# Compressed units first in the first attention, no identity products in its steady part, and eight dot-product tiles moved to the first feed-forward

## The chip, the cores and the metric

One core of one Trainium2 chip runs the whole program. The metric is the device time of one execution in microseconds (us); three executions of the kernel before are known. Engines are named as in the profile: PE is TensorE, DVE VectorE, ACT ScalarE, POOL GpSimd, SP the SyncE queue that issues the DMAs.

## The reference, cut to what matters

The program is two blocks. The first is one hybrid attention layer over 512 tokens; the second is two layers (feed-forward, mixer, feed-forward) over 512 + 256 tokens, modulated by vectors that come from a condition.

```python
# first block, for one layer
o_cmp, p_cmp = compressed_branch(qn, kc_cmp, vc_cmp)   # 31 compressed keys
o_sel = selected_branch(qn, ks_r, vs, sel_idx)
o_win = window_branch(qn, kw_r, vw)
o_nsa = (g0 * o_cmp + g1 * o_sel + g2 * o_win) * silu(z_n)
o_dsa = dsa_branch(qd, kd, v_d, qi_r, ki_r, wi) * silu(z_d)  # top 128 keys by an index score
x = x + concatenate([o_nsa, o_dsa]) @ w_out

# second block, for layer i
m  = split(silu(c)     @ w_ada[i] + b_ada[i], 9)       # 9 vectors of 1024
mc = split(silu(c_ctx) @ w_ada[i] + b_ada[i], 9)
h  = h + 0.5 * m[2] * swiglu(rms_norm(h) * (1 + m[1]) + m[0], w13, w2)
...
```

## The kernel before, in words

Each engine has its own instruction list and runs it strictly in order; semaphores tie them. Blocks end with a barrier of all engines. The blocks that the change touches come in this order: `compress` makes the compressed keys and values, `index_scores` makes the scores of the last branch (dsa), `attend_first` is the attention, `first_out` projects, and the first call of `ffn` follows.

**The attention** works through 16 units. A unit is one tile of 128 queries with one branch, for 8 heads. The branches cmp, sel and win of tile 3 come first, then those of tiles 2, 1 and 0, then the four dsa units. A unit has `items`, one for each group of 4 heads and each tile of 128 keys; a cmp unit has two, of 32 keys. For an item PE makes two products of 512 columns (three with a mask), `score`; ACT takes the exponential; PE multiplies with the values, 4 products, `weigh`. `weigh` of the item before is woven between the products of `score`. The row maxima must be there first: PE makes the rows (`row`, one product for each head, or 8 small ones in one go for a cmp unit), DVE reduces them (`maxes`), PE transposes the maxima (`turn`), ACT moves them (`move`), POOL spreads them (`spread_max`). Rows are made three units ahead: those of the first three units in a prologue, those of unit i+3 during unit i, shared out over its items, through two PSUM banks in turn (`wait_bank`), so that row j+2 waits until DVE has reduced row j.

DVE runs for each unit i: `finish(i - 1)`, `maxes(i + 3)`, then `rounds_at[i]` rounds of `topk` (48 rounds in all: 16 each for scores of 256, 384 and 512 keys; each round finds eight maxima and replaces them), then `share.vector`. Identity products (`keep_warm`) write to unused columns of PSUM: one after each row of the prologue, and one before the third product of each `weigh`.

**The modulation** vectors are dot products on DVE (`AdaShare`). A tile is 512 KB of `w_ada`, loaded to one of two buffers, and two products of 128x1024 (one for each condition); 72 tiles are one layer. 16 tiles are in `compress`, 8 in `attend_first`, 48 in the first `ffn`. `AdaShare.load` has SP wait, for tile n, until tile n-2 is done (`ada.SLOTS` is 2), and what SP has queued behind waits as well. `finish` adds the bias and the gain.

**The feed-forward** runs 34 steps, each of two weight loads of 512 KB. For step s ACT rounds the weights, DVE makes the rest (`rest_next`), PE multiplies. In iteration s DVE first makes the rest of step s+1, then takes the results of step s, then does its tiles of the share. On SP the order is: weights of step s, then the share's tiles of step s-1, then the weights of step s+1.

Of the kernel before, what the change touches and what calls it, by code (L numbers as in the profile page):

```python
# [6 lines left out]
P = 128  # L7
# [835 lines left out]
def compress(c, T, KKc, KLc, Vc, dram, share):  # L843
# [9 lines left out]
    with scope(nc) as sb:  # L853
# [14 lines left out]
        with nc.Block() as block:  # L868
# [22 lines left out]
            def _(pe):  # L891
# [14 lines left out]
                for g in range(GROUPS):  # L906
                    for ht in range(HT):
                        last = nc.tensor.matmul(c.PS[0:CMP_PAD, 5, g * HD:(g + 1) * HD], hid[:, 1, ht, g, :], w2[:, 1, ht, :], start=(ht == 0), stop=(ht == HT - 1))
                last.then_inc(out_done.sem, 1)
                pe.wait_ge(normed.sem, 1)  # L910
                for g in range(GROUPS):
# [67 lines left out]
def index_scores(c, rows, Q, KK, KL, scores, tri, sc_at, dram):  # L979
# [4 lines left out]
    with scope(nc) as sb:  # L984
        R = sb("ix_r", [P, 2, SEQ])
        wi = sb("ix_w", [P, QT, IDX_HEADS])
        with nc.Block() as block:
# [5 lines left out]
            def _(pe):  # L993
                for n, (t, h) in enumerate(items):
                    if n >= 4:
                        pe.wait_ge(relu.sem, n - 3)
                    keys = (t + 1) * P
                    tok = slice(t * P, (t + 1) * P)
                    half = slice(HD * (h % 2), HD * (h % 2) + HD)
                    q = HEAD_AT["qi"] + h  # L1000
                    nc.tensor.matmul(c.PS[:, n % 4, 0:keys], Q[:, q, tok], KK[:, KI_AT, 0:keys], start=True, stop=False)
                    nc.tensor.matmul(c.PS[:, n % 4, 0:keys], Q[half, q, tok], KL[half, KI_AT, 0:keys], start=False, stop=True
                                     ).then_inc(scored.sem, 1)

            @block.scalar
# [39 lines left out]
def attend_first(c, sb, rows, O, Q, KK, KL, KKc, KLc, Vx, Vc, scores, sc_at, tri, dram, share):  # L1045
# [5 lines left out]
    nc = c.nc  # L1051
    units = [FirstUnit(t, b) for t in range(QT - 1, -1, -1) for b in ("cmp", "sel", "win")] + [FirstUnit(t, "dsa") for t in range(QT)]
    n_units = len(units)
    rounds_at = [3, 8, 8, 2, 6, 6, 2, 4, 4, 1, 2, 2]
    rounds = [(t, r) for t in range(1, QT) for r in range(TOPK // 8)]
# [46 lines left out]
    with nc.Block() as block:  # L1102
        @block.sync
        def _(sp):
            sp.dma_start(negeye[:], dram["neg_eye"]).then_inc(tabs, 16)
            sp.dma_start(cneg[:], dram["cmp_neg"]).then_inc(tabs, 16)
            for i in range(n_units):
                share.load(sp, i)
            ring = Ring(c)
# [3 lines left out]
        def _(pe):  # L1113
# [51 lines left out]

            def keep_warm(bank, first=False):
                nc.tensor.matmul(c.PS[:, bank, 3 * P:4 * P], c.ident[:], c.ident[:], start=first, stop=True, skip_group_check=True)

            def weigh(n):
# [5 lines left out]
                for h in range(PER_GROUP):  # L1175
                    if h == 2:
                        keep_warm(o_bank(i, g))
                    if u.branch == "cmp":
# [8 lines left out]
                yield  # L1187

            for i in range(3):
                for j in range(units[i].row_items):  # L1190
                    row(i, j)
                    keep_warm(4 + j % 4, True)
                if i >= 1:
# [117 lines left out]
        def _(dve):  # L1311
            ch = c.dve.on(dve)

            def maxes(i):
# [3 lines left out]
                for j in range(u.row_items):  # L1318
                    dve.wait_ge(rowed, row_first[i] + j + 1)
                    ps = c.PS[:, bank("row", i, j), 0:u.keys]  # L1320
                    if u.branch == "cmp":
                        ps = c.PS[:, bank("row", i, j), 0:HEADS * CMP_PAD].rearrange("p (h c) -> p h c", h=HEADS)
                        ch.link(nc.vector.tensor_tensor(Sc[:], ps, cneg[:, u.t, None, :].to_broadcast([P, HEADS, CMP_PAD]), ALU.add))
                        nc.vector.reduce_max(Mx[:, i % 3, :, 64:68], Sc[:].rearrange("p (g h) c -> p g h c", g=GROUPS), AX_X).then_inc(maxed, 1)
# [48 lines left out]
            for i in range(n_units):  # L1373
# [4 lines left out]
                if i < len(rounds_at):  # L1378
                    for n in range(done, done + rounds_at[i]):
                        topk(n)  # L1380
                    done += rounds_at[i]
                share.vector(dve, ch, i)
            finish(n_units - 1)
# [367 lines left out]
class AdaShare:  # L1751
# [46 lines left out]

    def finish(self, dve, ch):

        ada, nc = self.ada, self.ada.nc
        if not self.finish_list:
            return
        dve.wait_ge(ada.small_in, 32)
        dve.wait_ge(ada.done, self.tiles[-1].stop)
        mods = [(l, v, m) for l, m in self.finish_list for v in range(2)]
        at = lambda l, v, m: ada.c.mod[:, l, v, m * KT:(m + 1) * KT]
# [12 lines left out]
def first_block(c, dram):  # L1820
    nc = c.nc
    O = c.hT.rearrange("p k n -> p (k n)")[:, 0:QT * D].rearrange("p (t n) -> p t n", t=QT)
    with scope(nc) as sb1:
# [9 lines left out]
        with scope(nc) as sb2:  # L1833
            KKc, KLc = sb2("KKc", [P, GROUPS, CMP_PAD], F32R), sb2("KLc", [P, GROUPS, CMP_PAD], F32R)
            Vc = sb2("Vc", [CMP_PAD, GROUPS, 66])
            s_c, room = sb2("ada_s", [P, 2, D]), sb2("ada_room", [P, 3, D])
            share = AdaShare(c.ada, s_c, [room[:, 0], room[:, 1]], room[:, 2], [2] * 8, [])
            compress(c, T, KKc, KLc, Vc, dram, share)
# [4 lines left out]
            with scope(nc) as sb:  # L1843
                later = AdaShare(c.ada, s_c, share.bufs, share.product, [0, 1, 1, 0, 1, 1, 0, 0, 0, 0, 0, 0, 1, 1, 1, 1], [(0, m) for m in range(3)], share)
                attend_first(c, sb, rows, O, Q, KK, KL, KKc, KLc, Vx, Vc, scores, sc_at, tri, dram, later)

# [152 lines left out]

def ffn(c, sb, ring, x, w13, w2, gates, spans, tag, after=None, shares=None, finish=()):  # L2000

# [48 lines left out]
    with nc.Block() as block:  # L2050
# [111 lines left out]
        def _(dve):  # L2162
# [5 lines left out]
            def body(s1, f0, is_up, i, more, opened=False):  # L2168
                for s, half, q, k in two(s1, i):
# [25 lines left out]
                    if share:  # L2195
                        share.vector(dve, c.dve.on(dve), s - s0)

            x.vector(dve, c.dve.on(dve), ring.rest_second(dve, s0))
# [570 lines left out]

def ada_shares(up, down):  # L2770

    out = []
    for f in range(0, FT, 8):
        out += [up] * min(8, FT - f) + [down if f == 0 else 0] * (KT // 2)
    return out


ADA_PLAN = {(0, 0): (ada_shares(2, 1), [(0, m) for m in range(3, 9)]),
            (0, 1): ([1] * 24, [(1, m) for m in range(3)]),
# [161 lines left out]
```

## Time and profile before

| | us |
|---|---|
| median of 3 executions | 3452.81 |
| lowest, highest | 3432.56, 3461.04 |
| the profiled execution, its own time | 3457.02 |
| its span (first to last instruction) | 3454.9 |
| mean granted TensorE clock | 0.935 |

Everything below is read from the profiled execution. A time without a unit is in us from the start of the span; the granted clock is 1.00 at 2.4 GHz and 0.50 at 1.2 GHz.

### The profile page before, as it was taken

Reading aid. Unit: us, or ns where it says so; the run is one execution under the profiler, and the core shown is the slowest. Engines: PE = TensorE matmul, PEld = TensorE weight load, DVE = VectorE, ACT = ScalarE, POOL = GpSimd, SP = SyncE. Lnnn points to the kernel's source line nnn. Section 1 sums busy time; section 2 is a strip of 40 time slices with the busy share of each in tenths; the row PEclk is TensorE's granted clock in tenths of the full one; section 3 lists DMA queues with packets and bytes.
Section 4 is the critical chain, followed back from the end, with each engine's and each line's share of the span. In section 5 each row is a group of like instructions: output and inputs, shape, how many; then the busy total and the mean of one; then the engine's idle time right before and its main releaser. Section 6 shows DMA issues by size and latency. Waiting matters only on the chain. (4 is left out here: it accounts for less than half of the span.)

```text
span 3454.9 us, 43440 instructions
## 1 busy us (share of the span) xinstructions
PE 3259.5 (94%) x18372; PEld 2819.4 (82%) x18372; DVE 1803.5 (52%) x2690; ACT 839.4 (24%) x1019; POOL 127.1 (4%) x96
## 2 busy tenths in 40 slices
PE   7847989899999999989999999999999999899999
PEld 6746878788888888668888888888888886699997
DVE  4656464276463663653644543664654556554434
ACT  3312222241121231222311212321211132132222
POOL 2320122000000000000000000000000000000000
PEclk9975555899999999999999999999999999999999
DMA  4332001234242412112333221343433320233331
GB/s 140 91 117 89 13 13 37 86 113 149 81 130 75 125 52 62 29 54 62 104 103 91 91 74 58 89 128 103 122 110 85 94 60 17 69 92 94 92 89 58
DMA packets 340322, 288.36 MB, mean 83 GB/s; under 512 B 12896, under 2 KB 315488, under 8 KB 339168
## 3 DMA queue, kind: packets, MB, share of 16 engines
q1 hardware_dynamic: 340192, 286.58, 28.3%
q8 instruction: 88, 1.44, 0.2%
q14 instruction: 42, 0.34, 0.0%
HBM read 279.72 MB, written 2.10 MB: 82 GB/s over the span
## 5 line engine op out<-in xcount | busy, mean ns | idle before, releaser
L2117 PE MATMUL PS<-x_hi_f,w_lo 128*128 128x258 f32 (+2 forms) x2560 | 622.3, 324 | 0.0
L2117 PE MATMUL PS<-x_lo_f,w_hi 128*128 128x258 f32 (+2 forms) x2560 | 622.0, 324 | 0.0
L2117 PE MATMUL PS<-x_hi_f,w_hi 128*128 128x258 f32 (+2 forms) x2560 | 620.9, 323 | 0.8 <-DVE w_lo L2165 0.8
L2117 PEld LDWEIGHTS PS<-x_hi_f,w_hi 128*128 128x128 f32 x2560 | 395.4, 189 | 43.9 <-issue 1.5
L2117 PEld LDWEIGHTS PS<-x_hi_f,w_lo 128*128 128x128 f32 x2560 | 395.3, 189 | 42.0
L2117 PEld LDWEIGHTS PS<-x_lo_f,w_hi 128*128 128x128 f32 x2560 | 393.2, 189 | 40.5
L2132 ACT ACTIVATE w_hi<-w_raw 128x2048 fp32r<-128x2048 f32 x131 | 250.0, 1909 | 498.6 <-PE PS L2117 496.7
L2117 PE MATMUL PS<-hid_hi_f,w_hi 128*128 128x512 f32 x1232 | 341.7, 347 | 0.9 <-DVE hid_lo_f L2185 0.9
L2117 PE MATMUL PS<-hid_hi_f,w_lo 128*128 128x512 f32 x1232 | 341.3, 347 | 0.0
L2117 PE MATMUL PS<-hid_lo_f,w_hi 128*128 128x512 f32 x1232 | 338.9, 345 | 0.0
L2165 DVE TENSOR_TENSOR w_lo<-w_raw,w_hi 128x2048 fp32r<-128x2048 f32 x131 | 299.6, 2287 | 35.1 <-ACT w_hi L2132 35.1
L2143 ACT ACTIVATE silu_a_f<-silu_a_f,shift_out_f 128x512 f32<-128x512 f32 (+1 forms) x154 | 90.2, 626 | 927.9 <-DVE silu_a_f L2176 927.9
L1793 DVE SCALAR_TENSOR_TENSOR sq_f<-sq_f,ada_s 128x1024 f32<-128x1024 f32 x240 | 293.5, 1223 | 8.8
L2192 DVE SCALAR_TENSOR_TENSOR hT<-PS,mod,hT 128x512 f32<-128x512 f32 (+1 forms) x168 | 95.8, 630 | 372.5 <-PE PS L2117 372.5
L2175 DVE COPY shift_out_f<-PS 128x4 f32<-128x4 f32 x88 | 14.3, 162 | 448.2 <-PE PS L2117 444.4
L2117 PEld LDWEIGHTS PS<-hid_hi_f,w_hi 128*128 128x128 f32 x1232 | 195.6, 188 | 33.0 <-DVE hid_lo_f L2185 2.3
L2117 PEld LDWEIGHTS PS<-hid_lo_f,w_hi 128*128 128x128 f32 x1232 | 194.9, 188 | 32.0
L2117 PEld LDWEIGHTS PS<-hid_hi_f,w_lo 128*128 128x128 f32 x1232 | 196.3, 188 | 28.9
L1182 PEld LDWEIGHTS PS<-first_v,exp_t 128*128 128x128 f32 x480 | 140.9, 331 | 11.7
L1182 PE MATMUL PS<-first_v,exp_t 128*128 128x66 f32 x480 | 123.5, 376 | 0.0
L2185 DVE TENSOR_TENSOR hid_lo_f<-hid_f_f,hid_hi_f 128x768 fp32r<-128x768 f32 (+1 forms) x88 | 78.5, 892 | 84.0 <-ACT hid_hi_f L2146 84.0
L139 PEld LDWEIGHTS PS<-ident 128*128 128x128 f32 x812 | 97.0, 196 | 20.0 <-issue 19.1
(325 smaller groups left out, 4607.1 us busy)
## 6 DMA issues: line engine op xcount, KB each, us to landing
w_raw<-in_w_ffn_dram SPq DMA_DIRECT2D x240, 512.0 KB, 5.1
sq_f<-in_w_ada_dram SPq DMA_DIRECT2D x120, 512.0 KB, 3.6
w_raw<-in_w_in_dram SPq DMA_DIRECT2D x46, 512.0 KB, 5.0
ada_room<-in_w_ada_dram SPq DMA_DIRECT2D x24, 512.0 KB, 3.5
w_raw<-in_w_out_dram SPq DMA_DIRECT2D x24, 512.0 KB, 5.2
w_raw<-in_w_ffn_dram SPq DMA_DIRECT2D x32, 384.0 KB, 3.9
ada_s<-in_conditions_dram SPq DMA_DIRECT2D x4, 1024.0 KB, 5.4
hT<-hT SPq DMA_DIRECT2D x56, 64.0 KB, 2.0
```

Of the source, the lines that this page charges most:

```text
L139: self.nc.tensor.matmul(self.PS[:, bank, 0:P], self.ident[:], self.ident[:], start=True, stop=True)
L1182: last = nc.tensor.matmul(c.PS[:, o_bank(i, g), h * 66:(h + 1) * 66], e, v, start=(kt == 0 and h == 0), stop=(kt == u.tiles - 1 and h == P ...
L1793: dot = nc.vector.scalar_tensor_tensor(self.product, self.bufs[n % ada.SLOTS], 1.0, self.s[:, v], ALU.mult, ALU.mult, accum_out=ada.c.mod[ ...
L2117: last = nc.tensor.matmul(c.PS[:, 4 * q + 2 * w + m, 0:e - a], wt, xt[:, a:e], start=first, stop=end)
L2132: nc.scalar.activation(ring.hi[:, q, :], ring.raw[:, q, :], ACT.Copy).then_inc(ring.rounded, 1)
L2143: last = nc.scalar.activation(sa[:, q, a:e], sa[:, q, a:e], ACT.Silu, bias=cc[:, q, 0, v:v + 1])
L2165: nc.vector.tensor_tensor(ring.lo[:, q, :], ring.raw[:, q, :], ring.hi[:, q, :].bitcast(F32), ALU.subtract).then_inc(ring.split, 1)
L2175: nc.vector.tensor_copy(cc[:, q], c.PS[:, 4 * q + 1:4 * q + 4:2, n_tok - cut:n_tok - cut + n_sh])
L2185: nc.vector.tensor_tensor(hid_lo[:, 2 * i + k, :], hf[:, q, :], hid_hi[:, 2 * i + k, :].bitcast(F32), ALU.subtract).then_inc(h_split.sem, 1)
L2192: last = nc.vector.scalar_tensor_tensor(c.hT[:, d, a:e], res(q, w)[:, a:e], gate[:, d:d + 1], c.hT[:, d, a:e], ALU.mult, ALU.add)
```

## The change

1. The four cmp units come first, then sel and win of tiles 3 to 0, then dsa. `rounds_at` goes from 3, 8, 8, 2, 6, 6, 2, 4, 4, 1, 2, 2 to none in the four cmp units and then 9, 10, 6, 7, 4, 4, 4, 4.
2. The identity product in `weigh` goes. In the prologue there are four after each row item, where there was one; since all three units there are cmp now, there are three row items and not 17.
3. 36 identity products stand in `compress` before PE waits for the normed keys, and 14 at the end of `index_scores`.
4. `attend_first` has no tile of the modulation; its eight are done in the first `ffn`, three in each of the first eight steps instead of two. The vectors 0 and 1 are finished at the end of the attention, vector 2 in step 3 of the `ffn`.
5. In `maxes` DVE waits for its own earlier maxima before it reuses `Sc`.

```diff
                 last.then_inc(out_done.sem, 1)
+                c.keep_warm(36, 7)
                 pe.wait_ge(normed.sem, 1)
...
                                      ).then_inc(scored.sem, 1)
+                c.keep_warm(14, 7)
...
-    units = [FirstUnit(t, b) for t in range(QT - 1, -1, -1) for b in ("cmp", "sel", "win")] + [FirstUnit(t, "dsa") for t in range(QT)]
+    units = [FirstUnit(t, "cmp") for t in range(QT - 1, -1, -1)]
+    units += [FirstUnit(t, b) for t in range(QT - 1, -1, -1) for b in ("sel", "win")] + [FirstUnit(t, "dsa") for t in range(QT)]
-    rounds_at = [3, 8, 8, 2, 6, 6, 2, 4, 4, 1, 2, 2]
+    rounds_at = [0, 0, 0, 0, 9, 10, 6, 7, 4, 4, 4, 4]
...
-            for i in range(n_units):
-                share.load(sp, i)
...
                 for h in range(PER_GROUP):
-                    if h == 2:
-                        keep_warm(o_bank(i, g))
...
                     row(i, j)
-                    keep_warm(4 + j % 4, True)
+                    for b in range(4, 8):
+                        keep_warm(b, True)
...
+                        if i >= 1:
+                            dve.wait_ge(maxed, row_first[i])
...
-                share.vector(dve, ch, i)
             finish(n_units - 1)
             share.finish(dve, ch)
...
-            share = AdaShare(c.ada, s_c, [room[:, 0], room[:, 1]], room[:, 2], [2] * 8, [])
+            share = AdaShare(c.ada, s_c, [room[:, 0], room[:, 1]], room[:, 2], [2] * 8, [(0, 0), (0, 1)])
...
-                later = AdaShare(c.ada, s_c, share.bufs, share.product, [0, 1, 1, 0, 1, 1, 0, 0, 0, 0, 0, 0, 1, 1, 1, 1], [(0, m) for m in range(3)], share)
...
                         share.vector(dve, c.dve.on(dve), s - s0)
+                        if soon and s - s0 == soon[0]:
+                            share.finish(dve, c.dve.on(dve), soon[1])
...
-        out += [up] * min(8, FT - f) + [down if f == 0 else 0] * (KT // 2)
+        out += [first if first and f == 0 else up] * min(8, FT - f) + [down if f == 0 else 0] * (KT // 2)
...
-ADA_PLAN = {(0, 0): (ada_shares(2, 1), [(0, m) for m in range(3, 9)]),
+ADA_PLAN = {(0, 0): (ada_shares(2, 1, 3), [(0, m) for m in range(3, 9)], (3, [(0, 2)])),
```

## Rows read from the trace of the kernel before

**Rows 1.** The page: the granted clock in 40 slices of the span

```profile
PEclk9975555899999999999999999999999999999999
```

**Rows 2.** Busy time by stretch (start:end, length, engines, granted clock, DMA share, GB/s)

```profile
330.20:343.60 13.40, 10.77 (x57) 7.47 (x55) 6.92 (x20) 8.65 (x14) 5.21 (x6) 1.00 0.00 1
...
408.60:412.00 3.40, 3.40 (x22) 2.52 (x21) 3.19 (x11) 1.84 (x4) 1.98 (x2) 0.99 0.00 0
...
542.00:624.60 82.60, 80.66 (x296) 71.03 (x295) 29.28 (x66) 15.83 (x27) 15.29 (x10) 0.50 0.15 39
```

**Rows 3.** Waits of PE from 345 to 626: who for whom, total, times, longest

```profile
PE PS L1124 <- DVE row_max L1333: 12.4, 8, 3.6
PE PS L1132 <- DVE row_max L1324: 7.0, 2, 4.0
```

**Rows 4.** Timeline of PE, 303 to 339 (start, length, instruction, idle before)

```profile
303.56 0.42 PE L912 MATMUL PS<-ident,cmp_r 32*128 32x32 f32 x2 [13.86 <-DVE cmp_r L969]
...
321.61 1.86 PE L1121 MATMUL PS<-KKc,Q 128*128 128x32 f32 x8 [1.74 <-PEq L987]
...
338.07 0.48 PE L1158 MATMUL PS<-Q,KKc 128*32 128x512 f32 x1
```

**Rows 5.** Timeline of PE, an item of the steady part

```profile
355.36 0.63 PE L1167 MATMUL PS<-ident 128*128 128x128 f32 x2
355.78 0.96 PE L1182 MATMUL PS<-first_v,exp_t 128*128 128x66 f32 x4
356.49 0.77 PE L1158 MATMUL PS<-Q,KK 128*128 128x512 f32 x1
357.07 0.53 PE L1182 MATMUL PS<-first_v,exp_t 128*128 128x66 f32 x2
```

**Rows 6.** Timeline of all engines, ACT and POOL in the prologue

```profile
327.69 3.90 ACT L1252 ACTIVATE first_rows<-first_rows 128x1024 f32<-128x1024 f32 x4
...
332.78 0.38 ACT L1233 ACTIVATE row_max_t<-PS 4x256 f32<-4x256 f32 x1
...
333.23 2.03 POOL L1278 TENSOR_TENSOR qr<-row_max_t,neg_eye 4x512 fp32r<-4x512 f32 x2 [113.37 <-ACT row_max_t L1233]
```

**Rows 7.** Timeline of DVE: last round on 256 keys, a tile, then finish

```profile
381.21 0.43 DVE L1338 MAX8 top<-scores 128x8 f32<-128x256 f32 x1
...
382.19 1.22 DVE L1793 SCALAR_TENSOR_TENSOR ada_room<-ada_room,ada_s 128x1024 f32<-128x1024 f32 x1
...
384.61 0.20 DVE L1349 RECIPROCAL co<-PS 128x8 f32<-128x8 f32 x1
```

**Rows 8.** Timeline of PE: its wait behind them

```profile
386.39 0.69 PE L1124 MATMUL PS<-KK,Q 128*128 128x384 f32 x1 [3.62 <-DVE row_max L1333]
```

**Rows 9.** Timeline of DVE: the starts of two rounds on 512 keys

```profile
492.11 0.69 DVE L1338 MAX8 top<-scores 128x8 f32<-128x512 f32 x1
...
493.63 0.69 DVE L1338 MAX8 top<-scores 128x8 f32<-128x512 f32 x1
```

**Rows 10.** Timeline of DVE: steps 1 and 3 of the first feed-forward

```profile
733.22 0.15 DVE L2175 COPY shift_out_f<-PS 128x4 f32<-128x4 f32 x1
...
767.52 0.16 DVE L2175 COPY shift_out_f<-PS 128x4 f32<-128x4 f32 x1 [4.30 <-PE PS L2117]
...
777.79 2.29 DVE L2165 TENSOR_TENSOR w_lo<-w_raw,w_hi 128x2048 fp32r<-128x2048 f32 x1
...
784.39 0.16 DVE L2175 COPY shift_out_f<-PS 128x4 f32<-128x4 f32 x1 [4.31 <-PE PS L2117]
```

**Rows 11.** Timeline of SP's queue, the same steps (start, from the first issue to the last)

```profile
775.29 2.95 SPq L1781 DMA_DIRECT2D sq_f<-in_w_ada_dram  x2
778.28 1.06 SPq L2061 DMA_DIRECT2D w_raw<-in_w_ffn_dram  x2
```

**Rows 12.** Source view of the feed-forward's weight loads (L2061), 726 to 850

```profile
DMA to landing us min/median/max: 5.0/5.8/6.9
```

**Rows 13.** Timeline of ACT, rounding of a step's weights

```profile
771.76 1.91 ACT L2132 ACTIVATE w_hi<-w_raw 128x2048 fp32r<-128x2048 f32 x1
```

More of the change, by code:

```diff
@@ L1164, in score @@
                 yield
-            def keep_warm(bank, first=False):
-                nc.tensor.matmul(c.PS[:, bank, 3 * P:4 * P], c.ident[:], c.ident[:], start=first, stop=True, skip_group_check=True)
             def weigh(n):
@@ L1187, in weigh, with keep_warm @@
                 yield
+            def keep_warm(bank, first=False):
+                nc.tensor.matmul(c.PS[:, bank, 3 * P:4 * P], c.ident[:], c.ident[:], start=first, stop=True, skip_group_check=True)
             for i in range(3):
@@ L1797, in vector, with finish @@
             dot.then_inc(ada.done, 1)
-    def finish(self, dve, ch):
+    def finish(self, dve, ch, some=None):
         ada, nc = self.ada, self.ada.nc
-        if not self.finish_list:
+        which = some or self.finish_list
+        if not which:
             return
         dve.wait_ge(ada.small_in, 32)
-        dve.wait_ge(ada.done, self.tiles[-1].stop)
-        mods = [(l, v, m) for l, m in self.finish_list for v in range(2)]
+        dve.wait_ge(ada.done, max(l * N_MOD * KT + (m + 1) * KT for l, m in which))
+        mods = [(l, v, m) for l, m in which for v in range(2)]
         at = lambda l, v, m: ada.c.mod[:, l, v, m * KT:(m + 1) * KT]
@@ L1843, in first_block @@
             with scope(nc) as sb:
-                later = AdaShare(c.ada, s_c, share.bufs, share.product, [0, 1, 1, 0, 1, 1, 0, 0, 0, 0, 0, 0, 1, 1, 1, 1], [(0, m) for m in range(3)], share)
-                attend_first(c, sb, rows, O, Q, KK, KL, KKc, KLc, Vx, Vc, scores, sc_at, tri, dram, later)
+                attend_first(c, sb, rows, O, Q, KK, KL, KKc, KLc, Vx, Vc, scores, sc_at, tri, dram, share)
 class Refill:
@@ L1997, in invert, with ffn @@
         ch.link(self.c.nc.vector.reciprocal(self.inv[:], self.inv[:]))
-def ffn(c, sb, ring, x, w13, w2, gates, spans, tag, after=None, shares=None, finish=()):
+def ffn(c, sb, ring, x, w13, w2, gates, spans, tag, after=None, shares=None, finish=(), soon=None):
     nc = c.nc
@@ L2767, in _, with ada_shares @@
                 sp.wait_ge(stored.sem, 16 * len(items))
-def ada_shares(up, down):
+def ada_shares(up, down, first=None):
     out = []
     for f in range(0, FT, 8):
-        out += [up] * min(8, FT - f) + [down if f == 0 else 0] * (KT // 2)
+        out += [first if first and f == 0 else up] * min(8, FT - f) + [down if f == 0 else 0] * (KT // 2)
     return out
-ADA_PLAN = {(0, 0): (ada_shares(2, 1), [(0, m) for m in range(3, 9)]),
+ADA_PLAN = {(0, 0): (ada_shares(2, 1, 3), [(0, m) for m in range(3, 9)], (3, [(0, 2)])),
             (0, 1): ([1] * 24, [(1, m) for m in range(3)]),
```

## The prediction

> **What bounds the kernel now.** I read the page's clock line first. TensorE has its full clock nearly everywhere except in the four slices from 259 to 605 us and at their edges [rows 1], and the first attention lies in the second half of that hole. Then the stretches. In the attention's last 82.6 us PE is busy for 80.66 at a clock of 0.50, which is 1.2 GHz; the clock is at 2.4 GHz only in the prologue and in short spells around a cmp unit [rows 2]. So the attention is bound by PE at half clock. What PE waits for there is DVE, and little of it: 12.4 us for row maxima of key tiles and 7.0 us, in two waits, for those of cmp units, 19.4 us together [rows 3]. The rest of the program, from 700 us on, is a feed-forward that PE bounds at full clock. There a step is 784.39 - 767.52 = 16.87 us, and DVE has 4.31 us of each step to spare [rows 10].
>
> **The change part by part.** Sums are made against the profiled execution: 3457.02 us, 2.1 of them outside its span. It stands 4.2 us above the median, 3452.81.
>
> *Identity products in compress.* PE idles 13.86 us before the transposes [rows 4]. One product (two records) takes 355.78 - 355.36 = 0.42 us at half clock [rows 5], so 36 take 15.1 us at that rate and half of it, 7.6, at the full one. The clock can't stay low through all of them if the prologue is a guide (it rose there while rows and identity products ran back to back), so they lie in the gap. Cost 0; up to 1.2 if the clock never rises. What follows them is idle again, so I give them no gain.
>
> *Identity products after the index scores.* 14 x 0.42 = 5.9 us, or 2.9 at full clock. PE's last product there ends 1.74 us before the attention's first [rows 4], and DVE covers most of that gap. The attention begins later by 1.5 to 4.7; I take +4.
>
> *The prologue.* Its length was the time from 321.61 to the first score at 338.07, 16.5 us [rows 4]. Three cmp rows replace 17 row items, so PE is done early, but it then waits. ACT does its four silu passes (327.69 to 331.59), the copy, and the first move, which ends at 333.16; POOL spreads it until 335.26 [rows 6]. That is 13.65 us after the block's start, and nothing in that chain is changed. So the first score comes 2.8 us sooner: -2.8. But PE stands idle for some 6 to 7 us just before the attention proper.
>
> *Identity products in weigh.* There are 8 items in the cmp units and 60 in the others, 68 in all: 68 x 0.42 = -28.6, since PE is the bound. Not all of it must arrive where DVE is late; that is counted below.
>
> *Rows.* The 16 rows of sel and win of tile 3 move out of the prologue into the cmp units, at 357.07 - 356.49 = 0.58 us for a product of 512 columns [rows 5]: +9.3. Two cmp rows go the other way, 1.7 each up to the next instruction (the row shows 1.86) [rows 4]: -3.4. Net +5.9.
>
> *The clock.* The attention loses spells at full clock: 5.5 us of the first one, from 338.07 to 343.6, and three of about 3.4 us [rows 2], 16 us in all. Each began as a cmp unit's scores were woven into a full item, which the new order hardly has. Work in them would take at most twice as long: 0 to +16, and since PE partly waited in them I take +6.
>
> *DVE's queue.* The case to read is unit 1. A round on 256 keys takes 382.19 - 381.21 = 0.98 us, the tile 2.42, and finish with the first row maximum 386.39 - 384.61 = 1.78 [rows 7, 8]. Eight rounds therefore began near 374.35, and PE's wait of 3.62 began at 382.77: PE covers 8.4 us before its third row of a unit needs DVE. Without identity products this cover is some 0.8 shorter, 7.6. A round on 512 keys takes 1.52 [rows 9]; for 384 I take 1.25, between the two. The wait after a unit is then rounds + 1.8 - cover. After unit 4 (9 rounds of 0.98) 3.0; after unit 5 (7 of 0.98, 3 of 1.25) 4.8; after unit 6 (6 of 1.25) 1.7. In tile 1 the third row comes one item, 2.9, sooner, cover 4.7: after unit 7 5.9, after unit 8 (4 of 1.52) 3.2. In units of two items the cover is about 3.8, so 4.1 each after units 9, 10 and 11. That is 30.9. In the cmp units DVE must reduce 24 rows in a short time; 4 us for that. 35 against 19.4 now: +15.5. Bounds: 0 (no more waits than now) and, with no cover at all, 60 + 8 x 1.8 = 74.4, which is +55. Taking the tile away is why this isn't worse: a tile stood ahead of each such finish.
>
> *The end.* One vector less (two of six additions and a scaling) is finished at the end, on the way to the barrier: -0.8 as an estimate, from DVE operations of 0.2 to 0.4 us like those around `finish` [rows 7]. The new wait on `maxed` is DVE's own last but one instruction: 0. The weights of `w_out`, no longer queued on SP behind tiles, come sooner, and nothing waits for them.
>
> So the attention gives 4 - 2.8 - 28.6 + 5.9 + 6 + 15.5 - 0.8 = -0.8 us. Nearly all that the identity products free is handed back.
>
> *Three tiles in a step of the feed-forward.* DVE's time alone would do: 2.6 us more in 4.31 spare. The queue of SP does not. Today, in the iteration that starts at 767.52, its first tile is done after 7.8 us, when the queue goes on at 775.29, and the two weight loads go out at 778.28 [rows 11]. In iteration j they are those of step j+3: the tiles ahead of them on SP are those of step j+1, which wait for the two tiles of iteration j. With three tiles, the third of step j waits for the first of the same step j, and behind it on SP stand the weights of step j+2, which PE wants 16.87 us after iteration j began. The chain in the new kernel: 7.8 (first tile done) + 0.4 (issue of the third) + 0.5 + 5.8 (second weight load issued, landed) [rows 12] + 1.9 (ACT rounds) [rows 13] + 2.3 (DVE's rest) [rows 10] + 0.1 = 18.8. DVE makes that rest before it takes the results of step j+1, so the chain closes on itself, and each step takes 18.8 instead of 16.87, +1.95. Step 0 is worse placed: its third tile is asked for only when the first is done, near 728.5, lands 3.6 us later at the least and ends near 734.8; with 2.3 for the rest, iteration 1 begins at 737.1 instead of 733.22 [rows 10], +3.9. Iteration 2 comes 5.3 late, and six more steps add 11.7: +17. PE is the bound afterwards and can't win it back. Bounds: +4, if loads land as fast as tiles do, in under 4 us; +23 with the longest landing, 6.9.
>
> Sum: 3457.0 - 0.8 + 17 = 3473 on the scale of this execution, 3469 on that of the median.
>
> **Rivals.**
> *A, the clock holds.* The cmp units, near which the clock moved, stand together at the start, and from sel of tile 3 on PE could run at 2.4 GHz. The work of the 60 items without identity products, about 60 x 3.0 = 180 us, would halve, while waits for DVE grow by some 25 as cover shrinks: about -65 to -80, total 3400, or 3396 on the median's scale. Against it speak two things. PE is idle for 6 us ahead of the first score, and before this change the clock fell in the cmp units. And afterwards it would have to rise out of a stream that is no denser than the one in which it stayed at 0.50 for 82.6 us [rows 2]. The Trainium skill, "TensorE: Matmul & The Clock Gate", section "Why this matters for your kernels", has it that a TensorE kept busy without gaps gets its full clock. By that rule the steady part would be warm, and rival A would be the forecast; here PE was busy for 98% of that stretch and was not.
>
> *B, slower.* The waits for DVE are not covered. It is decided by which instruction of PE first needs DVE in a unit: if it is the transposition of the maxima, as in the two waits of 7.0 us [rows 3], and not the third row, the cover is nil and the rounds stand bare: +55 in place of +15.5, 3473 + 39 = 3512, or 3508. For it: all 48 rounds now lie in eight units. Against: that transposition is for a unit whose rows DVE reduced before the rounds.
>
> *C, the weights come in time.* If SP isn't held, or loads land sooner, the +17 is 0 to +4: 3458, or 3454 on the median's scale. For it: the feed-forward has spare time on DVE and DMA. Against: the order of SP's list, which today's starts bear out.
>
> **How the numbers follow.** Forecast 0.59, A 0.14, B 0.09, C 0.16; 0.02 that the three executions shift by themselves more than they did (3432.56 to 3461.04, 0.8% wide). About 1%, 34 us, is what a measurement of this kernel can tell from no change. Faster by over 1% is A and little else: 0.15. Slower by over 1% is B and the upper end of the forecast: 0.12. Same: 0.73. The range: the forecast's terms reach from -16 (waits as now, identity products in full) to +30 around 3469 only if several go one way; C lies inside. I take 3425 to 3495, which leaves A and B out.
>
> **What would show it.** Granted clock 0.50 in the attention from its first scores on (A: 1.00). The first score 13.7 us after the block's first row. Items of about 2.9 us. PE's waits for row maxima near 35 us, the longest at the third row of the units of tile 1. In the feed-forward, starts of DVE's takes 18.8 apart in the first eight steps and 16.87 after, with ACT waiting for `w_raw`. The end of the attention near 624, that of the eighth step some 16 later than now. The prediction is wrong if the clock is full behind the cmp units, or if those eight steps still take 16.87.

## The result

The new kernel takes 3472.57 us in the median of 14 executions (3456.11 to 3477.87). The kernel before, run beside it on the same chip, takes 3432.38 in the median of 14 (3427.49 to 3461.04). The ratio is 1.009, interval 1.0066 to 1.0114: within 1%, close to the edge, and on the slow side. The forecast was 3469.

One fact is needed for every number below. The executions of the kernel before fall into two groups with nothing between them: of the 25 that the first experiments share, 13 lie at 3417 to 3436 and 12 at 3451 to 3461. The execution whose profile the prediction read, 3457.02, is of the upper group. The new kernel has 12 of 14 at 3469 to 3478 and 2 at 3456. So the two profiled executions differ by 19.3 us (spans 3474.2 and 3454.9; the forecast was +16), and the medians by 40. The median of a kernel with two groups lies in its larger group; the mean of the 14 executions, 3470.81 against 3440.18, differs by 30.6, which is what the ratio 1.009 says.

### The profile after, beside the rows of before

The page of the new kernel: PE's busy share and the granted clock in 40 slices. The low stretch covers the same four slices as in [rows 1].

```profile
PE   7848988899999999889999999999999999899999
PEclk9976555899999999999999999999999999999999
```

The stretches of the new kernel, to compare with [rows 2] (start:end, length, busy time of each engine, granted clock, DMA share, GB/s): the first part of the attention, the rest of it, and the first nine steps of the feed-forward.

```profile
341.00:400.00 59.00, 55.72 (x138) 30.52 (x139) 21.47 (x67) 14.47 (x25) 12.32 (x13) 0.50 0.00 1
400.00:622.00 222.00, 195.16 (x720) 172.98 (x718) 102.58 (x332) 49.93 (x86) 37.30 (x33) 0.50 0.00 0
720.00:872.00 152.00, 136.63 (x746) 117.72 (x745) 109.46 (x159) 31.86 (x33) 0.00 (x0) 0.97 0.45 140
```

The clock is 0.50 through the whole attention, without the short spells of [rows 2]. In the feed-forward PE is busy for 136.63 of 152 us. It is no longer the bound there. The 0.97 is two falls to half clock, of 6.8 and 3.4 us, where PE had waited for weights; DVE's takes of steps 1 to 7 come straight after its own rest (one waits 0.27 us for PE), so the falls don't set the length of a step.

Waits of PE from 345 to 628 in the new kernel, to compare with [rows 3]:

```profile
PE PS L1125 <- DVE row_max L1335: 25.7, 14, 4.1
PE PS L1125 <- ACT row_max_t L1233: 4.0, 5, 1.0
```

The two long waits of the maxima's transposition are gone. The waits at a row have grown from 8 to 14 and from 12.4 to 25.7 us; 11 of the 14 are at the third row that a unit makes.

PE's timeline in the new kernel, to compare with [rows 4, 8]:

```profile
305.09 0.42 PE L913 MATMUL PS<-ident,cmp_r 32*128 32x32 f32 x2 [5.92 <-DVE cmp_r L970]
...
321.33 5.87 PE L139 MATMUL PS<-ident 128*128 128x128 f32 x28
327.50 1.04 PE L1122 MATMUL PS<-KKc,Q 128*128 128x32 f32 x8 [0.30 <-PEq L988]
...
339.09 0.64 PE L1133 MATMUL PS<-ident,row_max 128*68 128x128 f32 x2 [5.09 <-ACT row_max_t L1233]
341.24 0.61 PE L1159 MATMUL PS<-Q,KKc 128*32 128x512 f32 x1 [1.51 <-ACT qr L1225]
...
430.47 0.58 PE L1125 MATMUL PS<-KK,Q 128*128 128x256 f32 x1 [3.13 <-DVE row_max L1335]
...
459.07 0.58 PE L1125 MATMUL PS<-KK,Q 128*128 128x256 f32 x1 [4.12 <-DVE row_max L1335]
```

In the first line PE is idle for 5.92 us, waiting for DVE, behind the 36 identity products of `compress` (13.86 us idle before): what the transposes wait for is DVE. The 14 identity products after the index scores take 5.87 us, nearly all at half clock, and the attention's block begins at 327.50, not 321.61. PE then idles 5.09 and 1.51 us ahead of its first score, which comes 13.74 after the block's start, as the forecast's chain through ACT and POOL had it (13.65). It was 16.46 before.

DVE's timeline in the feed-forward, to compare with [rows 10]: the takes of steps 0 to 3, and the rest made just before the last of them.

```profile
718.61 0.16 DVE L2176 COPY shift_out_f<-PS 128x4 f32<-128x4 f32 x1
...
734.28 0.16 DVE L2176 COPY shift_out_f<-PS 128x4 f32<-128x4 f32 x1
...
753.97 0.16 DVE L2176 COPY shift_out_f<-PS 128x4 f32<-128x4 f32 x1 [0.27 <-PE PS L2118]
...
771.11 2.29 DVE L2166 TENSOR_TENSOR w_lo<-w_raw,w_hi 128x2048 fp32r<-128x2048 f32 x1 [3.12 <-ACT w_hi L2133]
773.32 0.15 DVE L2176 COPY shift_out_f<-PS 128x4 f32<-128x4 f32 x1
```

SP's queue in the same step, to compare with [rows 11]:

```profile
761.75 0.33 SPq L1782 DMA_DIRECT2D sq_f<-in_w_ada_dram  x1
762.12 1.06 SPq L2062 DMA_DIRECT2D w_raw<-in_w_ffn_dram  x2
```

The source view of these two weight loads alone:

```profile
DMA to landing us min/median/max: 5.2/5.8/6.5
```

And ACT, to compare with [rows 13]:

```profile
769.16 1.91 ACT L2133 ACTIVATE w_hi<-w_raw 128x2048 fp32r<-128x2048 f32 x1 [10.85 <-DMA w_raw<-in_w_ffn_dram]
```

Together they show one turn of the new chain. The iteration begins at 753.97. SP gets past the wait for the first tile 7.78 us later and sends the third tile's load, then 0.37 later the first of the two weight loads. ACT, idle for 10.85 us, rounds those weights 7.04 after that issue (the second load goes out 0.48 after the first and lands 6.5 us later); DVE makes the rest and only then takes the next results, at 773.32. DVE now waits for ACT where it waited 4.3 us for PE before [rows 10].

### The profile page after: what moved, and what is told of

Read it like the earlier page. It is cut to its first block and busy times, and to the rows that moved or that the text cites. A ratio compares the mean times of both kernels' runs of the same rounds, so it can differ in the third digit from the quotient of the medians.

```text
span 3474.2 us, 43352 instructions
## 1 busy us (share of the span) xinstructions
PE 3261.3 (94%) x18326; PEld 2807.6 (81%) x18326; DVE 1799.0 (52%) x2690; ACT 839.9 (24%) x1019; POOL 123.3 (4%) x96
## 5 line engine op out<-in xcount | busy, mean ns | idle before, releaser
L1794 DVE SCALAR_TENSOR_TENSOR sq_f<-sq_f,ada_s 128x1024 f32<-128x1024 f32 x256 | 313.2, 1223 | 18.2 <-DMA sq_f<-in_w_ada_dram 9.2
L1178 PEld LDWEIGHTS PS<-first_v,exp_t 128*128 128x128 f32 x480 | 145.4, 331 | 15.5
L139 PEld LDWEIGHTS PS<-ident 128*128 128x128 f32 x912 | 113.2, 203 | 22.0 <-issue 21.1
L139 PE MATMUL PS<-ident 128*128 128x128 f32 x912 | 116.4, 287 | 15.5 <-PEq L426 6.7
```

Source lines behind the costliest of these rows:

```text
L139: self.nc.tensor.matmul(self.PS[:, bank, 0:P], self.ident[:], self.ident[:], start=True, stop=True)
L1178: last = nc.tensor.matmul(c.PS[:, o_bank(i, g), h * 66:(h + 1) * 66], e, v, start=(kt == 0 and h == 0), stop=(kt == u.tiles - 1 and h == P ...
L1794: dot = nc.vector.scalar_tensor_tensor(self.product, self.bufs[n % ada.SLOTS], 1.0, self.s[:, v], ALU.mult, ALU.mult, accum_out=ada.c.mod[ ...
```

## The experiments

Length of the attention is from PE's first score to the end of its last product with values. "Before" beside the first four runs (from "before again" on) has a median of 3435.72 (25 executions), beside the next four 3431.13 (26), beside the last three 3431.89 (17). These three rounds ran on three different chips. All ratios are against it; they compare the executions of each round and not the medians, so they need not be the quotient of the two medians.

| | median us (executions) | ratio, interval | attention, profiled |
|---|---|---|---|
| before, the profile read | | | 285.6 |
| after | 3472.57 (14) | 1.009, 1.0066 to 1.0114 | 280.8 |
| before again | 3432.48 (10) | 1.0005, 0.9959 to 1.005 | 259.9 |
| two tiles a step | 3447.84 (10) | 1.0037, 1.0 to 1.0073 | 261.0 |
| before without identity products | 3431.06 (10) | 0.9978, 0.994 to 1.0016 | 263.8 |
| after with them | 3494.47 (4) | 1.0192, 1.0134 to 1.0251 | 305.7 |
| old order | 3422.67 (10) | 0.995, 0.9918 to 0.9982 | 255.5 |
| one burst | 3408.22 (9) | 0.9905, 0.9871 to 0.9938 | 238.9 |
| only the tiles moved | 3441.08 (10) | 1.0041, 1.0001 to 1.0081 | 247.3 |
| filled prologue | 3465.01 (1) | | 277.9 |
| rounds spread | 3462.76 (10) | 1.0062, 1.003 to 1.0095 | 268.6 |
| burst at the first sel unit | 3472.54 (1) | | 274.8 |
| two bursts, rounds spread | 3395.27 (6) | 0.9866, 0.9819 to 0.9914 | 234.0 |

### The kernel before, again

No edit; its profile is what was wanted, since the times had fallen apart into two groups.

> The kernel before, run once more for a second profile. Its 14 executions lie in two groups, near 3430 and near 3457 us, and the profile that was read was one of the upper group. Theory 'clock': the lower group holds the full clock longer in the attention, so a profile from it has a mean clock above 0.935 and its attention (338 to 624.6 before) is about 25 us shorter, with more full-clock spells. Theory 'elsewhere': the 25 us lie outside the attention, whose length stays within 5 us of 286. The ratio to before is 1.00 either way.

This profile is of the lower group: 3431.9, 25.1 us less than the one read. Two stretches of its attention:

```profile
344.00:565.00 221.00, 194.16 (x740) 165.84 (x741) 126.13 (x383) 50.25 (x88) 40.28 (x37) 0.55 0.03 10
565.50:599.60 34.10, 32.49 (x228) 29.17 (x226) 13.93 (x25) 10.16 (x17) 9.77 (x6) 1.00 0.32 91
```

And PE's timeline where the second begins: the same two products of consecutive items, before and behind it.

```profile
564.16 0.77 PE L1158 MATMUL PS<-Q,KK 128*128 128x512 f32 x1
...
566.62 0.48 PE L1158 MATMUL PS<-Q,KK 128*128 128x512 f32 x1
```

The attention has a spell at full clock of 34.1 us in its last dsa units, in a stream in which the clock had stood at 0.50 since 470.0, with PE busy for 23.71 of the last 25 us, and in which the other execution [rows 2] stayed at 0.50 to the end. The attention is 285.6 - 259.9 = 25.7 us shorter. PE's waits for DVE are longer here, 24.9 against 19.4. The profile read was one without the spell. That the two groups are executions with and without it is read from these two profiles, and the mean granted clock of the others agrees: over 78 executions of the kernel before, the 48 of the lower group have 0.941 to 0.952 and the 30 of the upper one 0.932 to 0.939.

### Two tiles in a step again

```diff
-ADA_PLAN = {(0, 0): (ada_shares(2, 1, 3), [(0, m) for m in range(3, 9)], (3, [(0, 2)])),
+ADA_PLAN = {(0, 0): ([2] * 8 + [1] * 4 + [2] * 9 + [1] * 3 + [2] * 6 + [1, 1, 1, 0], [(0, m) for m in range(3, 9)], (3, [(0, 2)])),
```

The eight tiles stay in the feed-forward but are spread over later steps, at most two in each.

> The changed kernel with two tiles in each up step again, as before; the eight tiles go to down steps of the first feed-forward (2, 1, 1, 1 and 1, 1, 1, 0 in the second and third group of down steps). Theory 'queue' (the third tile holds the weights back on SP): the first eight steps take 16.87 again and the kernel gains 20 us on the changed one: 3452, ratio 1.003 to 1.007. Rival 'memory' (more DMA traffic and more DVE work in the feed-forward cost in themselves): the gain is under 8 us, ratio 1.009 or more.

DVE's takes of steps 1 to 3:

```profile
710.58 0.15 DVE L2176 COPY shift_out_f<-PS 128x4 f32<-128x4 f32 x1
728.00 0.16 DVE L2176 COPY shift_out_f<-PS 128x4 f32<-128x4 f32 x1 [4.97 <-PE PS L2118]
744.87 0.16 DVE L2176 COPY shift_out_f<-PS 128x4 f32<-128x4 f32 x1 [4.31 <-PE PS L2118]
```

A step takes 16.87 again, PE is what DVE waits for, and from the first take to the first result of step 8 it is 130.99 us; before 131.0, after 151.06. The median falls by 24.7; of this 20.1 lies before step 8, and the two profiles put another 2.8 behind it. The profile of this run also happened to hold a spell of 34.1 us in the last dsa units.

```profile
344.00:568.00 224.00, 194.12 (x649) 153.55 (x649) 121.10 (x389) 49.41 (x88) 41.66 (x38) 0.50 0.00 1
568.90:603.00 34.10, 32.49 (x196) 25.74 (x195) 3.95 (x15) 11.48 (x20) 5.88 (x6) 1.00 0.00 0
```

It is the lowest but one of the ten times, 3432.72; eight of them lie at 3446 to 3456. So the spell can also begin with no identity product near it, by the times more seldom than in the kernel before (2 of 10, with a mean clock of 0.941 and 0.943 against 0.933 to 0.937 of the rest).

### The kernel before without its identity products

```diff
                 for h in range(PER_GROUP):
-                    if h == 2:
-                        keep_warm(o_bank(i, g))
```

> The kernel before without the identity product in weigh, all else kept. Theory 'they hold the clock': the lower group of executions disappears, no full-clock spells are left beyond those after compressed units, and the time is 3440 to 3460 (ratio 1.002 to 1.008) although PE has 28.6 us less to do. Rival 'they are only work': 20 to 28 us faster than before, 3405 to 3412, ratio 0.992 to 0.994.

The profiled attention is at 0.50 from 344 to its end and takes 263.8 us: 21.8 less than the one read and 3.9 more than the one with the spell. Eight of the ten times lie at 3428 to 3439, two at 3413 and 3416. The median is 4.7 below before, inside the interval, and between what the two theories had stated; neither came out as it stood. The 21.8 us aren't the price of the products alone: this attention has 4.4 us at full clock, the one read 15.8. The reading, argued from the groups and not shown product by product: the identity products cost over 20 us in every execution, and some 6 in 10 get about as much back as a spell.

### The new kernel with identity products in its steady part

The same two lines put into the new `weigh`.

> The changed kernel with the identity product in weigh put back, all else kept. Theory 'they hold the clock': the steady part, with no compressed units in it, gets spells at full clock, and the time is the same or lower than the changed kernel's 3472, down to 3430. Rival 'they are only work': 15 to 28 us slower than the changed kernel, 3488 to 3500, ratio 1.016 to 1.020; the attention stays at 0.50 with items of 3.3 us instead of 2.9.

3494.47, 21.9 above the new kernel, and the attention takes 305.7 instead of 280.8. The only spell in it is one of 6.8 us near 427, and by their times, which agree within 9 us, the other three executions had no long one either. In these four executions of the new order identity products are nearly all work.

### The old order, with the tiles moved and no identity products

The version with two tiles a step, and in it the old lists of units and rounds and the old prologue; the 36 and 14 identity products are out as well.

```diff
-    units = [FirstUnit(t, "cmp") for t in range(QT - 1, -1, -1)]
-    units += [FirstUnit(t, b) for t in range(QT - 1, -1, -1) for b in ("sel", "win")] + [FirstUnit(t, "dsa") for t in range(QT)]
+    units = [FirstUnit(t, b) for t in range(QT - 1, -1, -1) for b in ("cmp", "sel", "win")] + [FirstUnit(t, "dsa") for t in range(QT)]
-    rounds_at = [0, 0, 0, 0, 9, 10, 6, 7, 4, 4, 4, 4]
+    rounds_at = [3, 8, 8, 2, 6, 6, 2, 4, 4, 1, 2, 2]
```

> The kernel before with three things taken from the change or from the run with two tiles: no identity product in weigh, no tile in the attention, and the eight tiles in down steps of the first feed-forward. Units, rounds and prologue are those of before. Theory 'order' (compressed units first cost 17 us by themselves: 16 rows leave the prologue for the steady part, and DVE's rounds bunch up): first score to last product of the attention takes 250 to 262 us where the changed kernel takes 281; time 3415 to 3425, ratio 0.994 to 0.998. Rival 'the order is harmless, the waits come from taking the tiles or the identity products away': 275 or more, and 3440 or more.

PE's waits in its attention:

```profile
PE PS L1122 <- DVE row_max L1329: 8.7, 7, 3.1
PE PS L1122 <- ACT row_max_t L1229: 3.4, 4, 1.1
```

3422.67, 25.2 below the version that differs from it in the order and its surroundings (eight of ten at 3421 to 3430, two at 3406 and 3407). The profiled attention takes 255.5, 25.3 less than the new kernel's, neither with a long spell: 29.7 - 12.1 = 17.6 of it are waits, and the forecast's 5.9 for rows that the new order has in PE's steady stream would be most of the rest. Its last stretch, and that of the new kernel:

```profile
540.00:596.00 56.00, 55.96 (x209) 50.41 (x207) 3.67 (x12) 12.38 (x21) 5.84 (x5) 0.50 0.00 0
```

The new kernel's:

```profile
566.00:622.00 56.00, 56.00 (x209) 50.52 (x207) 3.77 (x13) 12.38 (x21) 5.83 (x5) 0.50 0.00 1
```

These are the last 56 us of both attentions, the same products. PE is busy without a break, and at half clock.

### One burst of identity products where the long spell may begin

```diff
             for n, (i, g, kt) in enumerate(items):
+                if n == first[13]:
+                    for _ in range(14):
+                        keep_warm(o_bank(items[n - 1][0], items[n - 1][1]))
```

Into the old order of the run above, ahead of the second dsa unit.

> The same as the old-order kernel, with 14 identity products in one go ahead of the first item of the second dsa unit (tile 1). Theory 'a spell at full clock, once begun in the last units, lasts to their end' (two of the profiles show one of 34 us there, reached by chance): every execution has it, the attention is 15 to 20 us shorter than without the burst, the executions no longer lie in two groups, time 3400 to 3412, ratio 0.989 to 0.994. Rival 'the clock falls back at once': the burst costs its own 5.9 us, and the time is 3420 to 3430.

PE's timeline at the burst, and then the stretch behind it (columns as above):

```profile
538.27 4.79 PE L1183 MATMUL PS<-ident 128*128 128x128 f32 x28
542.81 0.48 PE L1156 MATMUL PS<-Q,KK 128*128 128x512 f32 x1
```

The stretch:

```profile
541.40:578.00 36.60, 35.72 (x223) 28.85 (x221) 2.89 (x9) 12.39 (x21) 5.86 (x5) 1.00 0.00 1
```

The clock rises inside the burst and stays at 2.4 GHz to the attention's last product. 4.8 us of identity products bring 16.6 us in the profile and 14.5 in the median, and all nine executions lie at 3402 to 3414, with a mean clock of 0.942 to 0.948 (0.937 to 0.940 in the eight slower ones without the burst): what came by chance comes each time.

### The kernel before with only the tiles moved

The tiles leave `attend_first` and go to the feed-forward three to a step, as in the new kernel; all else is the kernel before.

> The kernel before with nothing changed but the tiles: none in the attention, three in each of the first eight steps of the first feed-forward. Theory 'queue': DVE takes the results of those steps 19.35 us apart and the feed-forward loses 20.5 us; the attention gains up to 8 us from the absent tiles; ratio to before 1.003 to 1.006. Rival 'the loss in the feed-forward needs the new attention': steps of 16.87 and a ratio of 0.997 to 1.000.

The feed-forward takes 150.16 us to step 8, 19.2 more than before, so this cost belongs to the third tile and not to the new attention. The attention is 12.6 shorter than that of the kernel before with its spell (247.3 against 259.9): PE waits 8.1 less, as it would with no tile ahead of a row's maximum, and 4.5 us more of it are at full clock. The median is 10.0 above before, and the two groups are there again, each higher by about as much: six executions at 3431 to 3441, four at 3468 to 3470.

### The new prologue filled

```diff
                 if i >= 1:
+                if i == 2:
+                    for b in range(26):
+                        keep_warm(4 + b % 4, True)
                     turn(i - 1)
+                if i == 2:
+                    for b in range(8):
+                        keep_warm(4 + b % 4, True)
```

The diff is shortened: the first group stands ahead of the last `turn` of the prologue, the second behind it. It removes PE's idle time ahead of the first score, one of the two reasons that the prediction gave against rival A.

> The changed kernel with 34 more identity products in the prologue (26 ahead of the second transposition, 8 behind it), so that PE has no idle time of several us ahead of the first score. Theory 'the cmp units lose the clock': the clock is full at the first score and falls within the cmp units; sel and win run at 0.50, items of 2.9 us; time within 5 us of the changed kernel. Rival 'the idle time ahead of the first score loses it' (the forecast's first reason against its rival A): the clock stays full behind the cmp units, and the attention is 50 us shorter or more.

The stretch until the clock falls, and the one after:

```profile
322.40:342.90 20.50, 19.65 (x157) 17.66 (x156) 3.24 (x8) 14.71 (x22) 5.55 (x6) 1.00 0.42 106
342.90:615.00 272.10, 242.23 (x829) 197.76 (x829) 123.70 (x398) 60.57 (x105) 46.01 (x42) 0.50 0.00 1
```

The time, 3465.01, is 7.6 below the new kernel's median, where within 5 was expected; one execution can't price that. PE reaches the first score, at 338.02, at full clock and loses it 4.9 us later, among the short products of the cmp units, where its only gap is one of 0.23 us. Then it doesn't rise until the end. The idle time was there, but in this execution, the only one, it wasn't what kept the clock low.

### The new kernel with its rounds spread

```diff
-    rounds_at = [0, 0, 0, 0, 9, 10, 6, 7, 4, 4, 4, 4]
+    rounds_at = [2, 4, 4, 6, 8, 8, 4, 4, 4, 2, 1, 1]
```

> The changed kernel with the 48 rounds given to the units as 2, 4, 4, 6, 8, 8, 4, 4, 4, 2, 1, 1 instead of none in the four compressed ones. Theory 'DVE's queue' (rounds in front of the next row maxima make PE wait): PE's waits for row maxima fall from 25.7 to under 18 us, first score to last product from 281 to 266 to 272, time 3458 to 3464. Rival 'rounds in the compressed units only move the wait there': 278 to 284, and 3470 to 3476.

PE's waits in its attention:

```profile
PE PS L1125 <- DVE row_max L1335: 13.3, 11, 4.3
PE PS L1125 <- ACT row_max_t L1233: 4.0, 5, 1.0
```

The wait for DVE falls by 12.4 us, the attention by 12.2, the median by 9.8. In the new order the placement of the rounds is worth its wait, nearly one to one.

### A burst at the first sel unit of the new kernel

```diff
             for n, (i, g, kt) in enumerate(items):
+                if n == first[4]:
+                    for _ in range(18):
+                        keep_warm(o_bank(items[n - 1][0], items[n - 1][1]))
```

> The changed kernel with 18 identity products in one go between the last compressed unit and sel of tile 3. Theory 'once full, the clock holds through dense items and falls at DVE's first wait of several us': full clock in sel of tile 3, items of 1.6 to 1.8 us, and back to 0.50 in win or sel of tile 2, where PE waits for row maxima; the attention 3 to 8 us shorter, since waits take back much of the gain. Rival A of the forecast, given its start: full clock to the end of the units with few waits, 40 us or more shorter. Rival 'the clock falls within sel of tile 3': no change or 4 us longer.

Three stretches from the rise of the clock to its fall:

```profile
393.50:405.00 11.50, 11.50 (x79) 9.87 (x77) 3.43 (x12) 4.39 (x8) 2.03 (x2) 1.00 0.00 0
405.00:411.00 6.00, 6.00 (x44) 5.51 (x44) 2.78 (x9) 2.01 (x4) 0.00 (x0) 1.00 0.00 0
411.00:417.40 6.40, 3.57 (x27) 3.13 (x25) 5.95 (x20) 3.43 (x6) 2.03 (x2) 1.00 0.01 3
```

And what PE waited for behind it:

```profile
421.07 0.58 PE L1125 MATMUL PS<-KK,Q 128*128 128x256 f32 x1 [5.92 <-DVE row_max L1338]
```

The clock holds for 23.9 us of sel and win items and falls inside the wait that the first nine rounds cause (PE is idle from 415.15 to 421.07). So rival A's clock is possible for a time once it has been started, and here it ended in a wait that DVE's rounds cause. This is one execution; that such waits are what always ends it isn't shown. The feed-forward of this execution was also longer (152.23 to step 8), so its total, 3472.54, doesn't price the burst; the attention does, 6.0 less.

### Two bursts, and the rounds spread in the old order

Into the version with one burst:

```diff
-    rounds_at = [3, 8, 8, 2, 6, 6, 2, 4, 4, 1, 2, 2]
+    rounds_at = [6, 7, 6, 5, 5, 5, 3, 3, 2, 3, 2, 1]
...
-                if n == first[13]:
+                if n in (first[1], first[13]):
```

> The old-order kernel with the burst ahead of the second dsa unit, a second burst of 14 ahead of the first sel unit, and the rounds given as 6, 7, 6, 5, 5, 5, 3, 3, 2, 3, 2, 1. The waits for DVE decide when a spell ends, so fewer rounds in one go should let the first spell last through most of sel and win of tile 3: 10 to 18 us less than the kernel with one burst, 3392 to 3400, ratio 0.985 to 0.988. Rival (the second burst buys a spell that the first wait ends, and costs as much): 3405 to 3412.

PE's waits in its attention:

```profile
PE PS L1122 <- ACT row_max_t L1232: 3.7, 4, 1.1
PE PS L1122 <- DVE row_max L1332: 2.3, 5, 1.1
```

3395.27 is the best of all, 0.9866 of the kernel before and 2.2% below the new one (3395.27 / 3472.57 = 0.978). The gain over one burst is 13.0 in the median and 6.7 between the profiles. PE's waits for these maxima fall from 14.7 to 6.0, which is more than the 6.7 and less than the 13.0. So the time came out as expected, but not in the way expected: the burst that was added ran from 344.91 to 351.23, at half clock, the clock rose as it ended and fell 3.4 us later. Why it broke off, while the one in the new kernel held for 24, isn't settled. No run has the new rounds without this burst, so the two aren't priced apart.

## Why the prediction was right, and where it was not

*The attention's start.* Right. The clock rose inside the identity products in `compress` (at 292.4), and they ended 5.92 us before the transposes, so they cost 0, as taken. The transposes begin 1.5 later than before (305.09 against 303.56), but they wait for DVE, and in kernels without these products they begin anywhere from 300.8 to 305.6. The products after the index scores delay the block by 4.4 (from the transposes to the first row it is 22.41, and 18.05 in all profiles without them), where 4 was taken; the prologue gave back 2.7 for 2.8.

*The steady part.* Right in sum, partly by luck: the length fell by 4.8, where -28.6 + 5.9 + 6 + 15.5 = -1.2 was forecast, and two terms missed in opposite directions. The identity products were priced well. Counted from the end of the product before to the end of each, the 68 of the profile read take 28.7 us; the runs that take them out or put them back differ by 21.8 and 24.9 because their full-clock time differs too. PE's waits for row maxima are 25.7 and not 35, which is +6.3 (with those for ACT and the one for an exponential that is gone, 29.7 against 22.8: +6.9) in place of +15.5. That leaves some 17 us of added work for rows and the lost clock, where 5.9 + 6 = 11.9 was taken (-4.8 + 28.7 - 6.9 = 17.0). The waits lie where they were put, but the longest, 4.12, falls in the first unit of tile 2, where 4.8 was forecast; in the two units of tile 1, for which the cover was cut by 2.9, it is 3.98 and 1.03 for 5.9 and 3.2. So the cover was counted too thin there. That the term is real the spread rounds show, with 12 us for one line.

*The end of the attention.* Forecast near 624, measured 622.07 (before 623.62). From there to the first take of the feed-forward it is 0.7 less, for a forecast of 0.8, though this stretch lies between 95.5 and 97.2 over all profiles, so the agreement shows little.

*The feed-forward.* Right in its mechanism, which decides against rival C: the third tile's load waits for the first tile, the weights stand behind it on SP, and the two-tile plan takes it all away in either attention. The size was 20.1 to the first result of step 8, and 20.6 to the next take behind it, and not 17. A step takes 19.35 in the turn shown and 18.7 to 20.1 in steps 1 to 6, and not 18.8: the terms 7.8, 0.4, 1.9 and 2.3 came out as 7.78, 0.37, 1.95 and 2.21, but from the issue of the weights to ACT's start it is 7.04, not 0.5 + 5.8. The mis-sized term is the landing, 5.8 as the median of [rows 12]. That median mixes two kinds: of the two weight loads of a step the first lands 5.0 to 5.3 us after its issue and the second 6.4 to 7.2 (five steps, 726 to 822; before the change 5.0 to 5.2 and 6.3 to 6.9). ACT waits for the second. The longest step, 20.1, is the one whose second load took 7.15. The forecast's first steps are also not what its own terms give: 3.9 + 1.95 is 5.85 and not 5.3; measured, the second iteration began 5.55 late.

*The clock.* This is the step that failed: "The attention loses spells at full clock", 16 us in all, and "since PE partly waited in them I take +6". It priced the spells of one execution, 16 us with [rows 2], and called the rest of the attention a place where the clock stays low. Some 6 in 10 executions of the kernel before have a long spell just there, worth 25.7 us. In the new kernel 2 of 14 executions, with a mean clock of 0.94 against 0.931 to 0.936, seem to have one, worth 17 us. So against the kernel as it mostly runs the change lost another 20 us: 40 between the medians, less the 19.3 between the profiles; between the means it is 11. That the forecast in us came out near the mark is luck in this respect: it was built on an execution of the upper group; the change by medians, +40, is more than twice the +16 that it stated, and by means it is +31. That the three times shown were 0.8% apart was put down to chance with a weight of 0.02, while two of them, 3432.56 and 3461.04, are one of each group: a trace of one execution can't show what comes in some of them only.

*Adding up the medians.* Take the identity products out of before: -4.7. Move the tiles to the feed-forward, two a step: -8.4. New order, rounds, prologue and the products ahead of it: +25.2. The third tile in a step: +24.7. In sum +36.8 (the medians of before beside these runs differ by 4.6 at most, and the runs are of different chips). The first two edits pay, 13.1 together (ratio 0.995), though the first alone is inside its interval; the two others cost 49.9. By the ratios, which weigh both groups, the four are about -8, -10, +30 and +18, in sum +31. Both ways two edits gain and two lose; by the intervals each ratio's number is good to some 13 to 17 us, so the first two stand clear only together.

*Rival A* (the clock holds) failed: the clock is 0.50 from 336.8 on, ahead of the first score. The reason given first isn't the whole of it. In the filled prologue, one execution, the idle time before the first score is gone, and the cmp units lose the clock all the same. The second reason, that the clock would have to rise out of a stream no denser than one in which it stayed at 0.50, stands as a rule of thumb only: in three profiles it rose out of such a stream without a burst. The Trainium skill, "TensorE: Matmul & The Clock Gate", section "Why this matters for your kernels", has a TensorE that is kept busy without gaps run at its full clock. An unbroken burst of products bears that out (4.79 us of them, and the clock rose in it); the last 56 us of the new attention, busy for 56.00, don't. *Rival B* is refuted: with no cover the waits would be near 74, and they are 29.7.

## What to carry to other kernels

When the times given for a kernel lie 0.8% apart, read a profile of each end before pricing anything by one of them; a group of executions may have a whole stretch at another clock. Filler products spread over a loop cost their full time and leave the clock to chance; one unbroken burst, placed just ahead of a dense stretch that waits for nothing, cost 4.8 us here and made the gain come each time. Two bursts put elsewhere gave spells of 23.9 and 3.4 us only, so the place has to be tried. Before another item is added to a step because the engine that does it has time to spare, read the queue of the loads: a load that must wait for a buffer held back the loads behind it. And where a step needs two loads, price the later landing and not the median of both.

## What was not expected of the hardware

The clock depends on what went before. With PE busy for 55.96 of 56 us it stayed at 0.50, and over the same products, with one burst ahead of them, at 1.00 for 37.5 us. Spells of 34.1, 34.1, 37.5, 37.5 and 41.0 us were seen in the last units of five profiles, and each lasted until the attention's end or up to 4 us beyond; PE waits next to nothing there. Of the shorter ones, that of the burst at the first sel unit ended in a wait of PE (417.4) and that of the filled prologue among a cmp unit's short products (342.9). What starts a long one without a burst isn't settled. One profile has such a spell without identity products in `weigh`, and times some 16 us below the rest at a higher mean clock, in 9 of 54 executions of five such kernels, agree that it needs none; with them it was frequent in the old order, and in the new one (four executions) not seen.
